# Moving the second half of a merge and a threshold into the attention stage of a decoder layer

## What is computed

```python
h = rmsnorm(x, g_mix_pre)
q, k, v, q_idx, k_idx, w_idx, u = split(h @ w_in)
s = sum_h w_idx[h] * relu(q_idx[h] @ k_idx.T)        # index scores, 16 heads of 64
keep = top_k(s, 68 for the prompt, 256 for a sample) # which keys a query may see
a = softmax(q @ k[keep].T / sqrt(128)) @ v[keep]     # 8 heads, 2 key heads
p = causal mean over 2, 4, 8, 16 tokens of u, minus u, times pool_w
x = x + rmsnorm([a ; p] @ w_o, g_mix_post)
x = x + rmsnorm(conv_gated_ffn(rmsnorm(x, g_ffn_pre)), g_ffn_post)
```

## Time and profile before

| | |
|---|---|
| median of 3 runs | 1175.84 us (1175.38 to 1176.13) |
| the profiled execution | 1176.49 us, its span 1174.8 us |
| DVE, ACT, POOL busy | 801.5, 531.2, 73.4 us (68%, 45%, 6% of the span) |
| PE's clock, mean granted | 0.996 |
| chain that ended last | PE 90%, DVE 6%, ACT 2%, DMA 1% |

### The profile page before, as it was taken

One profiled execution on the slowest core, in us unless ns is written; L12 is line 12 of the kernel. 1 busy time (PEld: TensorE's weight loads), 2 busy tenths in 40 slices (PEclk: granted clock), 3 DMA queues, 4 the chain that ended last, 5 costly groups with the idle time before them and its releaser, 6 DMA issues.

```text
span 1174.8 us, 26065 instructions
## 1 busy us (share of the span) xinstructions
PE 1152.8 (98%) x9172; PEld 1117.6 (95%) x9172; DVE 801.5 (68%) x1489; ACT 531.2 (45%) x753; POOL 73.4 (6%) x98
## 2 busy tenths in 40 slices
PE   8999999999998999999999999999999999999998
PEld 8889999687996999999999999999999999999997
DVE  5667998765578787777777777777777544444443
ACT  7333333433346554545555554545455333333332
POOL 2730000032104000000000000000000000000000
PEclk9999999998999999999999999999999999999999
DMA  7677678877851655555555555555556766666651
GB/s 274 196 228 250 203 239 283 287 253 253 317 176 58 220 189 184 166 189 164 191 165 184 173 180 177 175 182 170 187 163 196 258 180 177 178 184 182 181 161 74
DMA packets 76856, 230.37 MB, mean 196 GB/s; under 512 B 9312, under 2 KB 24768, under 8 KB 75504
## 3 DMA queue, kind: packets, MB, share of 16 engines
q1 hardware_dynamic: 69392, 212.82, 56.7%
q10 hardware_dynamic: 4480, 9.01, 2.3%
q0 software_dynamic: 2944, 8.03, 2.0%
HBM read 223.25 MB, written 15.78 MB: 203 GB/s over the span
## 4 chain that ended last, share of the span: by engine, by line
PE 90%; DVE 6%; ACT 2%; DMA 1%; issue 1%; SPq 0%; POOL 0%; DVEq 0%; POOLq 0%
PE bank L1512 28%; PE bank L1513 28%; PE bank L1515 28%; DVE part L1381 1%; DVE lo L445 1%; DMA raw<-in_w_ik 1%; ACT hi L437 1%; PE bank L1728 1%; PE bank L1573 1%; DMA raw<-in_w_in 1%; DVE h_lo L1386 1%; PE bank L1885 0%; PE bank L1674 0%; ACT short L771 0%; ACT h_hi L664 0%
## 5 line engine op out<-in xcount | busy, mean ns | idle before, releaser
L1512 PE MATMUL bank<-h_hi,hi 128*128 128x266 f32 (+1 forms) x2096 | 604.2, 288 | 1.4 <-DVE lo L445 0.8
L1515 PE MATMUL bank<-h_hi,lo 128*128 128x266 f32 (+1 forms) x2096 | 602.6, 287 | 0.0
L1513 PE MATMUL bank<-h_lo,hi 128*128 128x266 f32 (+1 forms) x2096 | 601.8, 287 | 0.0
L445 DVE TENSOR_TENSOR lo<-raw,hi 128x1024 fp32r<-128x1024 f32 (+2 forms) x362 | 431.6, 1198 | 229.9 <-ACT hi L437 211.0
L437 ACT ACTIVATE hi<-raw 128x1024 fp32r<-128x1024 f32 (+2 forms) x362 | 373.1, 1034 | 273.2 <-PE bank L1515 238.5
L1512 PEld LDWEIGHTS bank<-h_hi,hi 128*128 128x128 f32 x2096 | 397.0, 189 | 9.2 <-issue 6.6
L1513 PEld LDWEIGHTS bank<-h_lo,hi 128*128 128x128 f32 x2096 | 395.6, 189 | 0.2
L1515 PEld LDWEIGHTS bank<-h_hi,lo 128*128 128x128 f32 x2096 | 395.3, 189 | 0.0
L1513 PE MATMUL bank<-g_lo,hi 128*128 128x264 f32 x704 | 200.5, 285 | 0.0
L1515 PE MATMUL bank<-g_hi,lo 128*128 128x264 f32 x704 | 199.6, 284 | 0.0
L1512 PE MATMUL bank<-g_hi,hi 128*128 128x264 f32 x704 | 199.4, 283 | 0.0
(11 more groups left out here) (283 smaller groups left out, 622.5 us busy)
## 6 DMA issues: line engine op xcount, KB each, us to landing
raw<-in_w_up SPq DMA_DIRECT2D x176, 512.0 KB, 3.9
raw<-in_w_in SPq DMA_DIRECT2D x56, 512.0 KB, 5.0
raw<-in_w_down SPq DMA_DIRECT2D x64, 448.0 KB, 3.5
raw<-in_w_o SPq DMA_DIRECT2D x32, 512.0 KB, 4.9
raw<-in_w_down SPq DMA_DIRECT2D x32, 512.0 KB, 3.7
kscr<-in_cache_k SPq DMA_DIRECT2D x64, 128.0 KB
mixed<-kscr SPq DMA_DIRECT2D x8, 512.0 KB, 7.5
cache_ring<-kscr SPq DMA_DIRECT2D x8, 512.0 KB, 9.3
```

Of the source, the lines that this page charges most:

```text
L445: ops.tensor_tensor(lo[:, s, 0:width], raw[:, s, 0:width], hi[:, s, 0:width].bitcast(F32), ALU.subtract).then_inc(done, 1)
L1512: mm(out, w_hi, x_hi[:, k, first:], start=(opens and done == 0), stop=False)
L1513: mm(out, w_hi, x_lo[:, k, first:], start=False, stop=False)
L1515: last = mm(out, w_lo, x_hi[:, k, first:], start=False, stop=(closes and done == total))
```

## The change

Four edits, in the order of the program:

1. PE does the products that turn the index weights, and the first scores of the first two index heads, between the two halves of the third index query tile, not behind it.
2. DVE takes a query tile out by three operations: the 8 sample columns go in one piece to `q_new`. After the scores of units 0 and 1 are masked, `turn_queries_of(0)` copies the first four heads' columns to `qbd` and `qnew` (four copies of 4 by 4 elements on 128 partitions), and after unit 0 is normalised `turn_queries_of(1)` those of the other four. PE's `sample_scores` waits for all eight copies (`q_turned`).
3. Compare steps 4 to 7 move from the last query tile into unit 0, the threshold into unit 1, `mask_above` from unit 1 to 2, and `mask_equal` from unit 2 to 3, where `mask_count` stays.
4. In each unit these parts stand ahead of the low half, not behind it.

```diff
@@ first_scores (tensor) @@
-            q_idx_tile(0, 2)
-            weights_turned()
-            for t in range(2):
-                pe.wait_ge(iq_ready, t + 1)
-                index_scores(2 * t, t)
+            def first_scores():
+                weights_turned()
+                pe.wait_ge(iq_ready, 1)
+                index_scores(0, 0)
+
+            q_idx_tile(0, 2, between=first_scores)
+            pe.wait_ge(iq_ready, 2)
+            index_scores(2, 1)
@@ query tiles (vector) @@
-                if h == 7:
-                    compare_quarters(4, 8)
-                    sample_threshold()
                 ps = tile_ready(t)
...
-                for dst in (to_bd, to_new):
-                    st.then(nc.vector.tensor_tensor(dst, by_round(ps[:, TP:T]), by_round(rms[:, TP:T]), mul))
+                st.then(nc.vector.tensor_tensor(q_new[:, h, :], ps[:, TP:T], rms[:, TP:T], mul))
@@ new, vector @@
+            def turn_queries_of(g):
+
+                heads = slice(g * HEADS // KV, (g + 1) * HEADS // KV)
+                src = q_new[:, heads, :].rearrange("p h (r j) -> p r j h", r=2)
...
+                for r in range(2):
+                    nc.vector.tensor_copy(to_bd[:, r, :, 32 * g + HEADS * r + 4 * g:32 * g + HEADS * r + 4 * g + 4],
+                                          src[:, r]).then_inc(q_turned, 1)
+                    nc.vector.tensor_copy(to_new[:, r, :, 4 * g:4 * g + 4], src[:, r]).then_inc(q_turned, 1)
@@ units (vector) @@
             masked_scores(1)
+            turn_queries_of(0)
             normalised(0)
+            turn_queries_of(1)
...
-                lo_chunk(dve, nc.vector, lo_dve, 0, C_WOP + 4 + u)
+                if u == 0:
+                    compare_quarters(4, 8)
                 if u == 1:
+                    sample_threshold()
+                if u == 2:
                     mask_above()
-                if u == 2:
+                if u == 3:
                     mask_equal()
-                if u == 3:
                     mask_count()
                 if u == 4:
                     mask_first()
                 if u == 5:
                     mask_whole()
+                lo_chunk(dve, nc.vector, lo_dve, 0, C_WOP + 4 + u)
@@ sample_scores (tensor) @@
+                pe.wait_ge(q_turned, 8)
```

More of the change, by code:

```diff
@@ L279, in build_program @@
     qlast = short[:, 3776:3904]
+    q_new = short[:, 3904:3968].rearrange("p (h b) -> p h b", h=HEADS)
     among = short[0:DB, 2240:2240 + CTX]
@@ L365, in build_program @@
     iq_turned = sem("iq_turned")
+    q_turned = sem("q_turned")
     relu_ready = sem("relu_ready")
@@ L1235, in _ @@
             lo_chunk(dve, nc.vector, lo_dve, 0, C_WOP + 1)
+            def turn_queries_of(g):
+                heads = slice(g * HEADS // KV, (g + 1) * HEADS // KV)
+                src = q_new[:, heads, :].rearrange("p h (r j) -> p r j h", r=2)
+                to_bd = qbd[:, 0:512].rearrange("p (r j x) -> p r j x", r=2, j=GROUPS)
+                to_new = qnew[:, g * P:(g + 1) * P].rearrange("p (j r c) -> p r j c", j=GROUPS, r=4)[:, 0:2]
+                for r in range(2):
+                    nc.vector.tensor_copy(to_bd[:, r, :, 32 * g + HEADS * r + 4 * g:32 * g + HEADS * r + 4 * g + 4],
+                                          src[:, r]).then_inc(q_turned, 1)
+                    nc.vector.tensor_copy(to_new[:, r, :, 4 * g:4 * g + 4], src[:, r]).then_inc(q_turned, 1)
             for j in range(8):
```

## The result

The changed kernel took 1168.72 us in the median of 4 runs (1167.04 to 1169.55), the kernel before 1175.61 on the same chip: a ratio of 0.9941 (95% interval 0.9923 to 0.9958). The forecast was 1168.0 us, and faster.

A forecast was written before the change was run, and what follows sets the result against it. PE bounds the kernel, busy 1152.8 of 1174.8 us, so only its waits can be won. Terms 1.0 + 1.85 - 0.1 + 5.05 = 7.8 off 1176.49 give 1168.7, median 0.65 lower: 1168.0 us, range 1166.3 to 1173.8.

The forecast's parts named there:

- First index scores: Before the second pair of index heads: PE's wait for ACT goes, gain 1.0 us, bounds 0 and 1.05.
- Last query tile: Between the pooling products: PE's 2.19 us wait for DVE's low halves goes, gain 1.85 us, bounds 1.5 and 2.19.
- The next thing late: Before the first attention scores: PE waits for the sixth pooling half, with the signals about 215.1.
- Queries turned once: Before unit 0's normalising: four copies on DVE, where it idles 0.31 us, loss 0.1 us, bounds 0 and 0.4.
- Mask parts ahead: Units up to the samples' softmax: parts fill DVE's 2.00 us idle before low halves, gain 5.05 us, bounds 0 and 7.6.
- The chain through the samples' softmax: DVE and ACT from unit 7 to the samples' normalising: ends at 276.85, where PE was at 281.89 before.
- the new wait: PE before the transposes of the samples' probabilities: 2 to 2.5 us in place of 0.56.
- One sign: Sign that the forecast is right: on DVE no idle over 1 us before units' low halves.
- The clock: Forecast: 1.00 from 262 to 290; rival: falls at the wait before the samples' transposes, costing 5.1, 1173.1 us, chance 0.27.
- What stands behind a wait: At the samples' transposes: transposes behind a wait do not count as busy, so the clock falls; full products did not.
- the sum: Whole kernel: 1.0 + 1.85 - 0.1 + 5.05 = 7.8 us gained.
- SP's queue as unchanged: Transfers: SP's queue is unchanged; 1.1 us later for a low half in unit 3 costs nothing.

The follow-up runs named there:

- the second experiment: The kernel before with only the mask parts of units 1 to 5 moved ahead of the low halves: 1169.9 us, 0.9964.
- the first experiment: The changed kernel with the parts of units 0 to 5 put behind the low halves again: 1174.56 us, 0.9993 to the kernel before.
- the second trace of the changed kernel: The changed kernel run once more with nothing changed, beside the last experiments: 1167.42 us, 0.9932 to the kernel before.

## Why the prediction was right

*First index scores*, 1.0: 0.94 measured: a lead of 0.76, and 0.18 that this execution had lost before, where both kernels are alike (13.16 against 13.34 at the index keys).

*Last query tile*, 1.85: 2.03. The 32 pooling products run in one piece. The next thing late is the sixth pooling half, as named; the wait for it is 0.46.

*Queries turned once*, a loss of 0.1: no loss. The step took four starts 0.08 apart plus the last one's end, and had 0.31 us of DVE's idle time to set against it; I should have let that cover all of it. The 0.28 won there is another's: the 0.39 us wait for unit 0's probabilities has gone, since DVE comes to the first masked scores 3.06 us earlier than before (219.07, 216.01) and PE to its first scores 2.79.

*Mask parts ahead*, 5.05: 5.30, as in the second experiment with this edit alone. The units of DVE, changed kernel:

```profile
253.65 0.42 DVE L1268 CUSTOM_DVE_ANT_0 short<-bank,W 128x256 f32<-128x256 f32 x1
253.99 0.08 DVE L1268 DVE_READ_ACCUMULATOR2_ANT mx<- 128x1 f32 x1
254.11 0.17 DVE L1272 TENSOR_SCALAR nmx<-mx 128x2 f32<-128x2 f32 x1
254.19 1.21 DVE L1131 TENSOR_TENSOR Ws<-Ws,short 8x1025 f32<-8x1025 f32 x1
255.43 0.68 DVE L1132 TENSOR_SCALAR Ws<-Ws 8x1025 f32<-8x1025 f32 x1
256.29 1.23 DVE L447 TENSOR_TENSOR lo<-raw,hi 128x1024 fp32r<-128x1024 f32 x1 [0.17 <-ACT hi L439]
257.43 0.43 DVE L1255 COPY part<-bank 128x266 f32<-128x266 f32 x1
...
261.71 1.23 DVE L447 TENSOR_TENSOR lo<-raw,hi 128x1024 fp32r<-128x1024 f32 x1 [2.00 <-ACT hi L439]
262.85 0.43 DVE L1255 COPY part<-bank 128x266 f32<-128x266 f32 x1
...
270.92 1.23 DVE L447 TENSOR_TENSOR lo<-raw,hi 128x1024 fp32r<-128x1024 f32 x1 [0.91 <-ACT hi L439]
```

Between the masked scores of unit 5, which end it at 254.11 + 0.17, and its low half the part now fills the time, and 0.17 of idle is left of 2.00. With the lead of 3.07 unit 6 begins at 257.43 + 3.07 = 260.50 on the old clock and unit 7 at 262.85 + 3.07 = 265.92; forecast were 260.5 and 265.95. The chain through the samples' softmax then ends at 273.52 + 3.07 = 276.59, forecast 276.85, and the new wait is 2.09 us, forecast 2 to 2.5. One sign was put wrongly: units 6 and 8 have no part, so the 2.00 us before unit 6's low half stay, and 0.91 before unit 8's.

*The clock.* In both traces of the changed kernel it stayed at 1.00 from 262 to 290, through the wait and the nine transposes behind it. The chance given to the fall was not idle, as the run with unit 5's part alone shows. Its price was too high for this order: where all parts stand ahead, each stretch at 1.2 GHz seen there lasts some 3.4 us, and most lie ahead of the wait, which takes them up. A stretch of 10.2 us stands only where the parts are behind, in the kernel before and in the first experiment, with waits of 1.89 and 2.46. What stands behind a wait, which the prediction offered as a reason, does not settle it: 2.09 and 2.20 us with nine transposes behind brought no fall, and 2.20 us with only full products behind brought one, in the run with the compare steps back.

*What the sum left out*: 0.99 us lost to the value pages, since the prediction counted SP's queue as unchanged and did not ask whether pages that start 8.4 us earlier also land 8.4 us earlier; and 0.5 won at 403.69. Both belong to this pair of traces: the second trace of the changed kernel does not wait for the pages, and the wait near 403 is 0 to 0.7 us in the other runs. At the samples' transposes the sum was 0.6 short (7.8 for 8.37), and these two took half a microsecond off, so that 7.8 met 7.9 is in part luck.

## What to carry over

Where an engine waits in every round of a loop for another one, put its independent work in front of that wait and not behind it: here that alone was worth 5.3 us in the trace and 4.2 to 5.0 in the time, and undoing it in the changed kernel undid the whole gain. Work each round out as a chain with its own period and compare it with PE's; the new wait then comes out in place, and in size where the clock stays up. When a stage is pulled in, ask of each transfer in it whether it lands as much earlier as it starts, and read that from more than one trace. Before holding one transfer back, look at what stands behind its consumer in every program.

## What was not expected

The clock falls in some executions and not in others at the same place of the same order. Behind a wait of PE it fell after 1.89, 2.20, 2.46, 2.50 and 4.02 us, and stayed up through 2.09, 2.11, 2.19, 2.25 and 2.43 and through another 2.20. It also fell with no wait just ahead: in six of the eleven traces with all mask parts ahead it was at 1.2 GHz for some 3.4 us from a point between 264 and 268, within 1.5 us behind the products that add the mask. In the other five it stayed at 1.00 there. Why is not shown, nor that the 1.89 us wait caused the stretch in the kernel before, which begins between 266 and 267. A wait just behind such a stretch hides it: 2.09 us became 0.59, and the time stayed the same.

A wait that a forecast is to remove can also vary with its order unchanged: the one at the last query tile was 2.19, 1.31 and 1.51 us.
